# Softmax attention in a fused two-layer inference step: the division moved behind the value product

## The reference, cut to what matters

```python
def sink_softmax(logits, sink):
    s = jnp.broadcast_to(sink[None, :, :, None, None], logits.shape[:-1] + (1,))
    p = jax.nn.softmax(jnp.concatenate([s, logits], -1), axis=-1)
    return p[..., 1:]
...
        s_c = jnp.einsum('bqkgd,bskd->bkgqs', qblk, ck, preferred_element_type=jnp.float32) * scale
        s_w = jnp.einsum('bqkgd,bskd->bkgqs', qblk, kw, preferred_element_type=jnp.float32) * scale
        s_w = jnp.where(ok, s_w, NEG_INF)
        p = sink_softmax(jnp.concatenate([s_c, s_w], -1), sink).astype(v.dtype)
        return (jnp.einsum('bkgqs,bskd->bqkgd', p[..., :P], cv)
                + jnp.einsum('bkgqs,bskd->bqkgd', p[..., P:], vw))
```

## Time and profile before

| what | value |
|---|---|
| median of 3 runs | 3066.55 us (3065.38 to 3067.62) |
| the profiled execution | 3057.68 us, its span 3055.9 us |
| PE busy | 2703.0 us (88%) |
| DVE busy | 1314.2 us (43%) |
| ACT busy | 1057.0 us (35%) |
| POOL busy | 189.6 us (6%) |
| mean granted TensorE clock | 0.94 |

### The profile page before, as it was taken

One profiled execution on the slowest core, in us unless ns is written; L12 is line 12 of the kernel. 1 busy time (PEld: TensorE's weight loads), 2 busy tenths in 40 slices (PEclk: granted clock), 3 DMA queues, 4 the chain that ended last, 5 costly groups with the idle time before them and its releaser, 6 DMA issues.

```text
span 3055.9 us, 72861 instructions
## 1 busy us (share of the span) xinstructions
PE 2703.0 (88%) x32894; PEld 2345.9 (77%) x32894; DVE 1314.2 (43%) x2266; ACT 1057.0 (35%) x1809; POOL 189.6 (6%) x155
## 2 busy tenths in 40 slices
PE   5998699997879999997977899987689999999996
PEld 3985577786679996447955677876589999999995
DVE  2346344443342220004454444533356555555665
ACT  3225334432332120013234434422344444444442
POOL 0001111110000000000000111101010000000010
PEclk8998799997989999998989899988799999999998
DMA  6212033210112221111200131000165555555571
GB/s 243 77 62 113 1 114 113 76 42 2 59 49 76 76 76 62 62 55 59 76 30 1 58 114 59 4 3 4 56 236 209 199 190 207 207 207 186 201 251 74
DMA packets 82717, 304.87 MB, mean 100 GB/s; under 512 B 9376, under 2 KB 9504, under 8 KB 82272
## 3 DMA queue, kind: packets, MB, share of 16 engines
q1 hardware_dynamic: 71072, 257.93, 23.5%
q0 software_dynamic: 11328, 42.21, 3.7%
HBM read 273.10 MB, written 27.00 MB: 98 GB/s over the span
## 4 chain that ended last, share of the span: by engine, by line
PE 84%; DVE 6%; issue 4%; ACT 4%; POOLq 1%; DMA 1%; DVEq 0%; POOL 0%; SPq 0%; PEldq 0%; ACTq 0%
PE ps L401 16%; PE ps L403 16%; PE ps L402 16%; PE ps L1178 6%; PE ps L965 3%; PE ps L978 3%; PE ps L958 3%; PE ps L842 2%; PE ps L641 2%; PE ps L724 1%; PE ps L414 1%; PE ps L781 1%; PE ps L766 1%; PE ps L870 1%; POOLq L2360 1%
## 5 line engine op out<-in xcount | busy, mean ns | idle before, releaser
L1784 DVE TENSOR_TENSOR ring_lo<-ring,w_ffn 128x1024 fp32r<-128x1024 f32 x308 | 374.1, 1224 | 217.2 <-ACT w_ffn L1371 211.3
L401 PE MATMUL ps<-hg_hi,w_ffn 128*128 128x256 f32 x1408 | 401.5, 285 | 0.9 <-DVE hg_lo L2224 0.9
L402 PE MATMUL ps<-hg_lo,w_ffn 128*128 128x256 f32 x1408 | 397.2, 282 | 0.0
L403 PE MATMUL ps<-hg_hi,ring_lo 128*128 128x256 f32 x1408 | 396.7, 282 | 0.0
L1371 ACT ACTIVATE w_ffn<-ring 128x1024 fp32r<-128x1024 f32 x308 | 322.3, 1056 | 198.1 <-PE ps L403 197.3
L401 PEld LDWEIGHTS ps<-hg_hi,w_ffn 128*128 128x128 f32 x1408 | 266.5, 189 | 2.5 <-DVE hg_lo L2224 1.1
L402 PEld LDWEIGHTS ps<-hg_lo,w_ffn 128*128 128x128 f32 x1408 | 265.6, 189 | 1.2
L403 PEld LDWEIGHTS ps<-hg_hi,ring_lo 128*128 128x128 f32 x1408 | 266.2, 189 | 0.0
L401 PE MATMUL ps<-hT_hi,w_proj 128*128 128x320 f32 x672 | 210.9, 314 | 10.0 <-DVE hT_lo L1790 10.0
L401 PE MATMUL ps<-hT_ffn_hi,w_ffn 128*128 128x320 f32 x704 | 214.3, 304 | 5.1 <-DVE hT_lo L1790 5.1
L402 PE MATMUL ps<-hT_lo,w_ffn 128*128 128x320 f32 x704 | 218.6, 310 | 0.0
(11 more groups left out here) (314 smaller groups left out, 5273.2 us busy)
## 6 DMA issues: line engine op xcount, KB each, us to landing
ring<-in_blocks SPq DMA_DIRECT2D x484, 512.0 KB, 3.5
h_rows<-arena POOLq DMA_DIRECT2D x16, 512.0 KB, 10.1
arena<-h_rows POOLq DMA_DIRECT2D x7, 1024.0 KB, 10.2
y_rows<-arena POOLq DMA_DIRECT2D x7, 1024.0 KB, 6.6
x<-in_x_all SPq DMA_DIRECT2D x1, 2560.0 KB, 13.1
h_plain<-arena POOLq DMA_DIRECT2D x1, 2560.0 KB, 11.5
out_y_all<-x POOLq DMA_DIRECT2D x5, 512.0 KB, 2.9
w<-in_low POOLq DMA_DIRECT2D x2, 768.0 KB, 4.9
```

What stands on the lines that cost most here:

```text
L401: nc.tensor.matmul(dst, w_hi, m_hi, start=start, stop=False)
L402: nc.tensor.matmul(dst, w_hi, m_lo, start=False, stop=False)
L403: return nc.tensor.matmul(dst, w_lo, m_hi, start=False, stop=stop)
L1784: V.tensor_tensor(ring_lo[:, n % RING, :], ring[:, n % RING, :], high[:, n % high.shape[1], :], ALU.subtract).then_inc(*E.sig("w_lo"))
```

## The change

- The probabilities are no longer divided before the value product. The product is made **token-major**: the turned probabilities are the weights (128 columns) and the values move (64 columns), so that the result has query tokens on the partitions. DVE then multiplies it by the reciprocals on its way out of PSUM (`out_norm`, into the new buffer `otok`), PE transposes it (`turn_out`) and DVE copies it to `oT` (`out_ev`).
- The four context units become two units of four heads (`N_CTXU = 2`); there are 18 units, and the latent ones begin at t = 2.
- DVE: the maxima of both heads are one instruction, the sums and reciprocals are those of unit t-2.
- PE: step t is now chunk 0 of t-2, the output's transposition of t-4, scores of t, chunk 1 of t-2, value product of t-3, chunk 2 of t-2.
- ACT: step t is now copy of chunk 0 of t-2, the exponential of the first head of t, copy of chunk 1, the exponential of the second head, copy of chunk 2.
- The context scores and the first two rotations stand ahead of the turning of caches; the other three rotations stand at t = 2, 5 and 9, each waited for by the first unit that needs it (`ROPE_BEFORE`). The sine product is made in PSUM. The copies of the turned caches move from DVE to ACT, behind the context's exponentials.

```diff
-        N_PAIRS = 4 * NT
+        N_CTXU = 2
+        N_ATT = N_CTXU + 16
+        ROPE_BANK = (2, 5, 2, 5, 5)
+        ROPE_AT = {2: 2, 5: 3, 9: 4}
+        ROPE_BEFORE = {2: 2, 4: 3, 7: 4, 11: 5}
...
             def turn_probs(l, t, k):
...
-                pe.wait_ge(sem["at_p"], 2 * n + (1 if z * P <= n_keys(blkq) else 2))
+                if k == 0:
+                    pe.wait_ge(sem["at_exp"], l * N_ATT + t + 1)
...
             def attend(l, t):
...
-                for j in range(m):
-                    for g in range(2):
-                        mm = nc.tensor.matmul(ps[rows64(g), 7, 0:P], value_op(g, kb[g][j]), probT[:, t % 2, g * nk + j * P:g * nk + (j + 1) * P],
-                                              start=j == 0, stop=j == m - 1)
+                at = value_cols(t).start
+                for h, (c, g) in enumerate(heads):
+                    kb = key_blocks(g, blkq)
+                    for j in range(m):
+                        mm = nc.tensor.matmul(ps[:, 7, at + h * HD:at + (h + 1) * HD], probT[:, t % 2, h * nk + j * P:h * nk + (j + 1) * P],
+                                              value_op(g, kb[j]), start=j == 0, stop=j == m - 1, skip_group_check=True)
...
+            def turn_out(l, t):
...
+                pe.wait_ge(sem["at_on"], first + t + 1)
+                at = turned_cols(t).start
+                for k in range(len(heads_of(t)) // 2):
+                    mm = nc.tensor.transpose(ps[:, 7, at + k * P:at + (k + 1) * P], otok[:, t % 2, k * P:(k + 1) * P], ident)
...
-                for t in range(N_PAIRS + 3):
-                    if t < N_PAIRS:
+                for t in range(2, N_ATT + 4):
+                    if t < N_ATT + 2:
+                        turn_probs(l, t - 2, 0)
+                    if t >= 4:
+                        turn_out(l, t - 4)
+                    if t < N_ATT:
                         scores(l, t)
-                    if 1 <= t <= 3:
-                        rope_turn(l, t + 1)
-                    if 2 <= t < N_PAIRS + 2:
-                        turn_probs(l, t - 2, 0)
+                    if t in ROPE_AT:
+                        rope_turn(l, ROPE_AT[t])
+                    if t < N_ATT + 2:
                         turn_probs(l, t - 2, 1)
-                    if 3 <= t:
+                    if 3 <= t < N_ATT + 3:
                         attend(l, t - 3)
-                    if 2 <= t < N_PAIRS + 2:
+                    if t < N_ATT + 2:
                         turn_probs(l, t - 2, 2)
...
             def att_phase(l):
-                act.wait_ge(sem["rope_ev"], 5 * l + 2)
-                for t in range(N_PAIRS + 2):
-                    if t >= 2:
-                        for k in range(3):
-                            probs_ev(l, t - 2, k)
-                    if t < N_PAIRS:
...
+                for t in range(N_ATT + 2):
+                    probs_ev(l, t - 2, 0)
+                    if t < N_ATT:
+                        act.wait_ge(sem["at_max"], l * N_ATT + t + 1)
...
+                        for h in range(len(heads_of(t)) - 1):
+                            probs(l, t, h)
+                    probs_ev(l, t - 2, 1)
+                    if t < N_ATT:
+                        probs(l, t, len(heads_of(t)) - 1)
+                    probs_ev(l, t - 2, 2)
+                    if t == 1:
+                        act.wait_ge(sem["kc_tr"], l + 1)
+                        A(kcT[:, :], ps[:, 6, 0:PAST], ACT.Copy).then_inc(*E.sig("act_step"))
...
+            def out_norm(l, t):
...
+                V.tensor_tensor(otok[:, t % 2, 0:n * HD].rearrange("p (h d) -> p h d", h=n),
+                                ps[:, 7, value_cols(t)].rearrange("p (h d) -> p h d", h=n),
+                                stat(t, 2).unsqueeze(2).broadcast_to([P, n, HD]), ALU.mult).then_inc(*E.sig("at_on"))
...
             def att_phase(l):
...
-                        for g in range(2):
-                            pr = prob[:, (t - 1) % 3, g * nk:(g + 1) * nk]
-                            V.tensor_scalar(pr, pr, a[:, 2, g:g + 1], None, ALU.mult).then_inc(*E.sig("at_p"))
...
+                    if t < N_ATT:
+                        dve.wait_ge(sem["at_s"], l * N_ATT + t + 1)
+                        V.tensor_reduce(by_tile(stat(t, 4)) if t < N_CTXU else stat(t, 4), scores_of(t), AX.X, ALU.max).then_inc(*E.sig("dve_step"))
```

More of the change, by code:

```diff
@@ L278, in build @@
         zeros = take(D)
-        ropetmp = take(512)
+        otok = take(2 * 2 * P, b=2, c=2 * P)
         cursor[0] = MIX_END
@@ L431, in with_flag, with heads_of, query_block, query_tiles @@
                 body()
-        N_PAIRS = 4 * NT
-        def pair_of(t):
-            return (t, -1) if t < 4 else ((t - 4) // 4, (t - 4) % 4)
+        N_CTXU = 2
[3 more added lines that the diff above has]
+        ROPE_BEFORE = {2: 2, 4: 3, 7: 4, 11: 5}
+        def heads_of(t):
+            if t < N_CTXU:
+                return [(2 * t + c, g) for c in range(2) for g in range(2)]
+            return [((t - N_CTXU) // 4, g) for g in range(2)]
+        def query_block(t):
+            return -1 if t < N_CTXU else (t - N_CTXU) % 4
+        def query_tiles(t):
+            c = heads_of(t)
+            return slice(c[0][0], c[-1][0] + 1)
         def own_blocks(blkq):
@@ L712, in scores, with put @@
             def scores(l, t):
[L714 to L715 removed]
+                heads, blkq = heads_of(t), query_block(t)
+                n = l * N_ATT + t
                 if t >= 2:
[L717 to L719 removed]
+                    pe.wait_ge(sem["at_exp"], n - 1)
+                if t in ROPE_BEFORE:
+                    pe.wait_ge(sem["rope_ev"], 5 * l + ROPE_BEFORE[t])
                 tok = slice((blkq + 1) * P, (blkq + 2) * P)
+                def put(h, at, rhs):
+                    c, g = heads[h]
+                    return nc.tensor.matmul(flat[:, at:at + rhs.shape[1]], qT[rows64(g), c, tok], rhs, start=True, stop=False, skip_group_check=True)
+                if blkq < 0:
+                    for h, (c, g) in enumerate(heads):
+                        mm = put(h, score_at(t, h), key_op(g, "ctx"))
+                    mm.then_inc(sem["at_s"], 1)
+                    return
+                c = heads[0][0]
                 own = own_blocks(blkq)
[L723 to L724 removed]
                 a0, a1 = score_at(t, 0), score_at(t, 1)
[L726 to L729, removed]
                 three = len(own) == 3
[L731 removed]
+                two = slice(CTX + own[0] * P, CTX + (own[0] + 2) * P)
                 def hide(g, b):
@@ L741, in scores @@
                 put(0, a0, kcT[rows64(0), :])
-                put(1, a1 + PAST, kT[rows64(1), two[0]])
-                put(0, a0 + PAST, kT[rows64(0), two[0]])
+                put(1, a1 + PAST, kT[rows64(1), two])
+                put(0, a0 + PAST, kT[rows64(0), two])
                 edge = own[0] if blkq > 0 else own[1]
@@ L2450, in _ @@
                 next_phase()
-                for c in range(5):
-                    dst = kT[:, CTX:T] if c == 0 else qT[:, c - 1, CTX:T]
-                    pool.wait_ge(sem["rope_mm"], 5 * l + c + 1)
-                    nc.gpsimd.tensor_tensor(dst, dst, C("cos"), ALU.mult).then_inc(sem["rope_cos"], 1)
+                rope_cos(l, 0)
+                rope_cos(l, 1)
                 pool.wait_ge(sem["kc_ev"], l + 1)
```

161 lines of the change are left out of this document (88 added, 73 removed).

## The result

| | before | after |
|---|---|---|
| median, us | 3066.91 (3065.38 to 3067.62) | 3137.99 (3132.77 to 3140.64) |
| ratio of the runs | | 1.023, interval 1.0213 to 1.0248 |
| profiled execution, us | 3057.68 | 3132.77 |
| mean granted clock | 0.940 | 0.925 |
| attention, layer 0, us | 114.0 | 144.1 |

The change costs 71 us, against +50 forecast. It is slower, within the range, and its median lies 21.5 above the forecast one. Between the profiled executions it costs 75.1: the stages take 288.7 instead of 225.5, +63.2, and 11.9 lie outside them.

A forecast was written before the change was run, and what follows sets the result against it. PE was taken to bound the kernel (84% of the span); longer attention rounds outweigh the earlier front, +21.5 us, plus 14 and 15 for low clock, making +50: 3116.5 us for the median, range 3080 to 3180.

The forecast's parts named there:

- front: Attention stage's start to first latent scores: two rotations and two context units ahead, 9 us, gaining 12 against 20.9.
- three filling rounds: Rounds t = 2 to 4 behind light context units: 2.7 + 5.3 + 7.0 = 15 us a stage at full clock.
- twelve rounds: Steady part of each stage: twelve rounds of 6.74 us, 80.9 us with PE at full clock.
- from the last scores to the end: End of each stage: 15.0 us before plus dearer value products, multiplication, transposition and copy, 18.6 us at full clock.
- clock, both stages, apart: Added for low clock: 14 us for four or five filling rounds in both stages, 15 us for five later rounds.
- ring: PE, DVE and ACT wait on each other once per unit; rounds of 6.50 and 6.98 us, 6.74 average, against 5.03.
- The product's pace: Value product on PE: 0.105 us an instruction at full clock, bounds 0.062 and 0.209; 1.7 or 2.1 us a unit.
- Slow rounds: Rounds at 1.2 GHz are bound by PE, 9.6 us, 2.9 over 6.74; five of the later 24 taken as slow.
- The stuck clock: Rival: clock stays down through most rounds, 28 of 36 slow in both stages; +110 us, 3177; chance 0.15.
- The opened ring: Rival: ACT's copies come without delay, PE's work is the round, 5.3 us; both stages -20, 3046 us; chance 0.08.
- The draw: Case of no change: front and longer rounds cancel if a round is near 5.9 us; 3066 us; chance 0.07.
- DVE's work: Two multiplications of 0.55 us per 640-key unit removed from DVE; by itself worth nothing in the steady part.

The follow-up runs named there:

- e1: Changed kernel with ACT's copies of chunks 0 and 1 of unit t-2 ahead of the wait for the maxima of t; 3086.98 us.
- e2: Changed kernel with PE's scores of unit t ahead of chunk 0 of t-2 and the output's transposition, ACT's order as changed; 3083.28 us.
- e6: Kernel before with only ACT's order of the change, copies of chunks 1 and 2 each behind an exponential; 3096.29 us.
- e5: Changed kernel with PE's scores ahead of chunk 0 and output transposition, and ACT's copies of chunks 0 and 1 ahead of the maxima's wait; 3075.57 us.
- e3: Changed kernel in its orders with the old value product (64-column weights), leaving out division, output multiplication and output transposition; 3081.68 us.
- e4: Changed kernel with five filler products per round on PE from unit 7 on, into a free bank, where PE waits; 3093.41 us.
- e10: Changed kernel, product and division kept, with PE's scores first, output transposition behind chunk 0, all ACT copies ahead of the maxima's wait; 3085.89 us.
- e9: Changed kernel with old product, DVE dividing t-1 behind the maxima of t, ACT's copies first, PE's product between chunks 0 and 1; 3031.96 us.

## Why the prediction was right, and where it was short

By stage, the profiled executions give (layer 0, layer 1):

| term | forecast | measured |
|---|---|---|
| front | 9 | 8.5, 9.0 |
| three filling rounds | 15 | 18.4, 17.8 |
| twelve rounds | 80.9 | 90.4, 91.0 |
| from the last scores to the end | 18.6 | 26.8, 26.8 |
| stage | 123.5 | 144.1, 144.6 |
| clock, both stages, apart | 14 + 15 | in the rows above, 41.7 |

- **What bounds, front, ring: right.** The front gained 12 us. The round at full clock was 26.1 for four units against 26.96 forecast, in the order of pieces that was written down, and e1, e2 and e6 show that it is a ring made by the two orders: cutting either link takes 2.4 to 3.5 us of each tile away, and ACT's order alone, put on the kernel before, closes it once a tile.
- **The product's pace: right.** Forecast 0.105 at full clock. In e5's chain 20 take 2.18, 0.109, and they are hidden in the change at full clock (e3's rounds differ by 0.11 only). At 0.50 it is 0.208, the bound that the key norm's row gave (0.209). The Trainium skill (TensorE: Matmul & The Clock Gate, LDWEIGHTS (loading the stationary operand)) gives 107 ns for 128 columns without naming a level of the clock: the trace agrees at 1.00 (0.109), and not at 0.50 (0.208).
- **Slow rounds: right in size and number, the two terms shared out wrongly.** Forecast 9.6 each and five of them; measured are five at 0.50 or 0.51 throughout (10.31 and 9.45 in layer 0, 10.05, 9.45 and 9.24 in layer 1). Eight more of the 24 had the low clock for a part, up to 8.38 us. Against their own full-clock sum (79.8 a stage with its two rotations) the later rounds lost 10.6 and 11.2, 21.8 where 15 were forecast; filling stands 3.4 and 2.8 above its 15, 6.2 where 14 were forecast. The sum of both, 28.0 against 29, is right because one miss covers the other.
- **The tail: the step that failed.** "From the last scores to the end 18.6" was reckoned at full clock, as if the last three products ran at the pace of the round. e4's tail, at a granted 0.98, takes 19.1, so the sum was nearly right at that level. In the change the windows of the tail have 0.59 and 0.60, with 4.16, 4.17 and 3.66 us for the last three products of layer 0: 8.2 us more than forecast in each layer, 16.4 together. I had read that before's tail took 15.0 and didn't ask at which clock this one would run, though each round now left PE waiting. Two of the three in the chain:

```profile
338.46 4.16 PE ps L823 x20
...
346.50 4.17 PE ps L823 x20
```

With this term the stages are accounted for: 21.5 forecast at full clock, -0.5 in the front, 6.2 in filling, 19.6 in the twelve rounds (measured less 80.9, both layers) and 16.4 in the tails make the 63.2 that were measured.
- **Outside the stages** 11.9 us were not forecast. The changed kernel's instructions there are the same. The span less both of PE's stages is 2828.0 us in the profiled execution of before, 2839.7 in that of the change, and from 2825.2 (e3) to 2842.8 (e10) in the other kernels; e6, whose stage lasts 128.1, has 2838.7. The loss comes behind each attention stage, in the recurrent half: PE's instructions there run 30.0 us behind before's at 349 us and 33.5 at 909, and 67.2 at 1707 and 74.7 at 2123. Outside the stages the change also has more time at 0.50, 336.6 us against 321.0, but e6 is nearly as dear with 322.0, so the clock isn't all of it. Before's profiled execution was itself 9 us under its median, and the change's 5 under its own. How much of the 11.9 is the spread between executions and how much the change brings about is open.
- **The rivals.** The stuck clock didn't come: the clock came back in every stage, and rounds at the ring's full-clock length stood beside the slow ones. But it was nearer than its chance of 0.15 says, with 131.5 us of the stages at 0.50 after 44.4. The second rule quoted, swings of the clock from small idle gaps of PE between groups of matmuls (the Trainium skill, TensorE: Matmul & The Clock Gate, A second HAM failure mode: psum-queue depth-cycling), is borne out in kind by e4: once the gaps were filled, the clock stayed at 1.00 in both layers nearly to the end of the tail. The opened ring wasn't the case either, and e5 shows that its price was too low: opened, the round is 5.7 and not 5.3, because PE's hole comes back with it. The draw, 5.9 a round, is thus about where e1, e2 and e5 came out (5.6 to 5.9), 3076 to 3087.
- **DVE's work** did fall by what was said, 1314.2 to 1280.7 us, and bought nothing.

## What to carry to other kernels

Before an order is changed, write down each ring of engines that it closes, one piece per row: here copies behind exponentials and scores behind a chunk cost 26.1 - 20.1 = 6.0 us a tile, although DVE had less to do and PE's own work (5.0 a round in e5) still fitted into the old pace. A ring leaves PE idle, and here idle PE cost a second time through its clock, so each later term (the tail too) has to be costed at both levels. In the faster version the division stands where its engine has slack and hardly anybody waits (on DVE, behind the next maxima), and the product where PE would wait for a copy. e9 and e10 differ in product and division together, so what the division's place alone is worth wasn't shown.

## What was unexpected of the hardware

- PE busy without a gap didn't by itself bring the clock back: 19.00 of 19 us busy at 0.50 with the 64-column product, against a return after one slow round (busy 8.55 of 9) with the 128-column one in e3. Which property of the product decides was not isolated.
- A small DVE operation of 2 columns, 0.16 us as a rule, took 0.98 in some places, here on the chain:

```profile
L1977 DVE TENSOR_TENSOR small<-small,sink x1: 981/981/981, 270.5 to 270.5; 128x2 f32<-128x2 f32 x1
```

The timeline shows with what. POOL's cosine product of a rotation runs from 270.20 to 271.47, and this operation, started at 270.50, ends at 271.48. The other long ones in the change's attention (0.79 to 1.27 us) also start while POOL works and end within 0.03 us of it. That is what a rotation costs the ring: 7.04 - 6.22 = 0.82, and 0.98 - 0.16 = 0.82. Not every small operation beside POOL's work is long, and no run moved the rotation away.
- The chain has 0.109 us an instruction for the token-major product in e5 and 0.121 in e10, both at 1.00. The pace is the same: from start to start 0.112 in both. In e5 the first product starts at 267.81, while the last transposition ahead of it runs until 267.97, and the chain counts the product from there; in e10 it starts behind a wait and nothing covers it. A price read from the chain depends on what stands ahead.
- With the old product two instructions, one of each head, start together: in the kernel before, their starts are 0.006 and 0.103 us apart in turn (from 259.31), which makes 0.109 for a pair. The token-major product needs 0.11 for each single one, though it moves half the columns.
